# Two Transformer blocks on one core: a second scratch place for the stick-breaking ring, the latent queries' work moved ahead of it, two more modulation tiles in the input projection, and GpSimd's queue no longer emptied in the gather stage

## What is computed

```python
# block 1
proj = rms(x) @ w_in                     # 2208 columns: sb_q, sb_k, sb_v, cq, ckv, k_pe
# stick-breaking attention, 8 heads of 64
z = q k^T / 8;  log_fail = where(s < t, log_sigmoid(-z), 0)
later = cumsum(log_fail, reverse) - log_fail
a = where(s < t, exp(log_sigmoid(z) + later), 0);  sb = a @ v
# latent attention, 8 heads: q = rms(cq) @ w_uq (96 wide), kv = rms(ckv) @ w_ukv
q, k = rms per head; the last 32 of each head turned by rope; softmax over chunks; @ v
x += [rms(sb), rms(mla)] @ w_o
# expert gather: per token 8 heads, top 16 x top 16 of 2 x 128 keys -> 16 experts per head
pre = x . u[idx];  x += sum(softmax(best) * gelu(pre) * v[idx])   # u, v: 16384 x 1024
# block 2
mod = silu(c) @ w_ada + b_ada            # w_ada: 1024 x 6144, one row of six vectors
x += g1 * (mixer(rms(x) * (1 + sc1) + sh1) @ w_out)   # forgetting, mLSTM and block attention
x += g2 * ((silu(gate) * up) @ w_down)
```

## Time and profile before

| | |
|---|---|
| median of 3 runs | 2475.4 us (2469.62 to 2479.81) |
| the profiled execution | 2482.66 us |
| its span, first to last instruction | 2480.7 us |
| mean granted clock of TensorE | 0.905 |
| busy share | PE 84%, DVE 69%, POOL 42%, ACT 25% |
| input projection and what stands before it | 0 to about 136 us |
| up-projection | about 136 to 178 us |
| ring | about 178 to 266 us |
| opening, to the first gather | 266 to 310 us |
| gather stage | 310 to about 1870 us |
| rest of block 2 | to 2480.7 us |

### The profile page before, as it was taken

The page is one execution under the profiler, slowest core; times in us unless marked ns, Lnnn a source line. Parts: engine busy times, 40 slices in busy tenths (PEclk is TensorE's granted clock), DMA queues, the critical chain, the costliest instruction groups (busy, mean ns, idle before and its releaser), DMA issues. The chain is left out here.

```text
span 2480.7 us, 25461 instructions
## 1 busy us (share of the span) xinstructions
PE 2081.8 (84%) x7721; PEld 1317.2 (53%) x7721; DVE 1706.0 (69%) x3528; ACT 610.8 (25%) x1443; POOL 1041.7 (42%) x1086
## 2 busy tenths in 40 slices
PE   7987878987776986877987977777888898999999
PEld 6955555544332343433543433333336874788887
DVE  7747487876877776777666787877856574544464
ACT  3134234432222121122112132222211231210121
POOL 0010066666666666666665666666670000000000
PEclk9985989998887998889999988988998998999999
DMA  7652089999999999999999999999995311333222
GB/s 272 226 196 76 18 307 341 358 366 363 328 330 401 352 371 400 406 387 384 365 403 349 403 397 356 354 362 357 370 376 182 113 44 43 93 101 94 75 86 101
DMA packets 260632, 676.43 MB, mean 273 GB/s; under 512 B 19501, under 2 KB 107938, under 8 KB 260514
## 3 DMA queue, kind: packets, MB, share of 16 engines
q0 software_dynamic: 147456, 536.94, 57.3%
q1 hardware_dynamic: 113058, 138.07, 16.6%
HBM read 672.81 MB, written 2.10 MB: 272 GB/s over the span
## 5 line engine op out<-in xcount | busy, mean ns | idle before, releaser
L2570 PE MATMUL bank<-arena 128*128 128x512 f32 x1568 | 831.9, 666 | 176.1 <-issue 73.2
L2791 DVE SCALAR_TENSOR_TENSOR arena<-arena,h_ps 128x1024 f32<-128x1024 f32 x512 | 612.5, 1217 | 168.0 <-DMA arena<-in_peer_u,arena 116.0
L2524 POOL DMA_INDIRECT arena<-in_peer_v,arena x512 | 512.5, 1001 | 336.1 <-issue 137.8
L2524 POOL DMA_INDIRECT arena<-in_peer_u,arena x512 | 510.1, 996 | 233.5 <-issue 144.3
L2570 PEld LDWEIGHTS bank<-arena 128*128 128x128 f32 x1568 | 311.2, 212 | 539.9 <-issue 428.6
L2805 DVE SCALAR_TENSOR_TENSOR x<-arena,x 128x1024 f32<-128x1024 f32 x120 | 154.4, 1287 | 42.4 <-DMA arena<-in_peer_v,arena 23.6
L2651 ACT ACTIVATE arena<-ident,arena 128x128 f32<-128x128 f32 x392 | 138.5, 393 | 88.9 <-issue 27.7
L142 DVE CAST parts<-arena 128x2048 fp32r<-128x2048 f32 (+5 forms) x61 | 67.6, 1107 | 93.7 <-DMA arena<-in_w_gate_up 75.2
L144 DVE TENSOR_TENSOR parts<-arena,parts 128x2048 fp32r<-128x2048 f32 (+5 forms) x61 | 125.4, 2056 | 4.5
L1605 PE MATMUL bank<-hT,arena 128*128 128x256 f32 (+1 forms) x576 | 122.0, 368 | 3.6 <-DMA arena<-in_peer_w_q 2.2
L1605 PEld LDWEIGHTS bank<-hT,arena 128*128 128x128 f32 x576 | 104.5, 201 | 30.1 <-issue 16.2
(11 more groups left out here) (476 smaller groups left out, 3268.5 us busy)
## 6 DMA issues: line engine op xcount, KB each, us to landing
arena<-in_w_ada SPq DMA_DIRECT2D x12, 2048.0 KB, 12.1
arena<-in_w_in SPq DMA_DIRECT2D x15, 1536.0 KB, 6.8
arena<-in_w_gate_up SPq DMA_DIRECT2D x44, 512.0 KB, 5.0
arena<-in_peer_w_q SPq DMA_DIRECT2D x16, 1024.0 KB, 7.8
arena<-in_w_down SPq DMA_DIRECT2D x22, 512.0 KB, 3.5
arena<-in_peer_u,arena POOLq DMA_INDIRECT x512
arena<-in_peer_v,arena POOLq DMA_INDIRECT x512
arena<-in_w_in SPq DMA_DIRECT2D x7, 1024.0 KB
```

The costliest lines, as they stand in the source:

```text
L2524: nc.gpsimd.indirect_dma_start(out=row, out_offset=None, in_=a[table][0], in_offset=bass.IndirectOffsetOnAxis(ap=expert[:, s % TB, j:j + 1 ...
L2570: ins = nc.tensor.matmul(psum[half][:, :], diag[:, m % R, :], row[:, half * 512:(half + 1) * 512], start=(s % PH == 0 and j == 0), stop=(s ...
L2791: nc.vector.scalar_tensor_tensor(out=u_ring[:, n % R, :], in0=u_ring[:, n % R, :], scalar=1.0, in1=h_ps[:, :], op0=ALU.mult, op1=ALU.mult, ...
```

## The change

1. `ADA_EARLY` goes from 8 to 10: the projection's tiles 3, 4 and 5 carry two `w_ada` tiles each; two are left for the up-projection. There SP issues them ahead of the expert keys, and neither waits for a used place.
2. The queries' work on DVE (`sum_q`, rope, `scale_q` of both groups) moves from the ring's slots to the end of `up_dve`; their root (`root_heads(act, 0)`) moves into `up_act`, behind its 13th sum.
3. The ring's scratch grows from 1024 to 1280 columns; `work0` has two places by turns, so `log_one_plus` waits for the `before_exp` of the unit before the last (group A; `att_b` keeps one).
4. For stick-breaking units of `att_a`, PE issues the scores ahead of the values and the turn in its slot; ACT takes both copies out of PSUM from DVE, and its order in a slot is now log, store, exponents, copy.
5. In the gather stage DVE clears `gate_of[0].bias`, POOL waits for that and does the `iota` alone; the `drain` is gone.

```diff
-        ADA_EARLY = 8
+        ADA_EARLY = 10
-        ADA_AT = {1: (0, 1), 2: (2, 3), 3: (4,), 4: (5,), 5: (6, 7)}
+        ADA_AT = {1: (0, 1), 2: (2, 3), 3: (4, 5), 4: (6, 7), 5: (8, 9)}
@@ up_sync
-            sync.dma_start(key_rows, ...).then_inc(keys_loaded, 16)
             for t in range(ADA_EARLY, ADA_TILES):
                 load_ada(sync, t)
+            sync.dma_start(key_rows, ...).then_inc(keys_loaded, 16)
@@ up_dve
                 ada_weigh(dve, t)
+            sum_q(dve)
+            for g in range(2):
+                turn_q_places(dve, g)
+                add_q_places(dve, g)
+            for g in range(2):
+                scale_q(dve, g)
@@ up_act
+                    if m == 3 * TB:
+                        root_heads(act, 0)
@@ att_places
-            p.work0, p.work1, p.probs, p.probsT = (scratch[:, i * p.n_max:(i + 1) * p.n_max] for i in range(4))
+            p.work1, p.probs, p.probsT, *p.work0 = (scratch[:, at:at + p.n_max] for at in range(0, scratch.shape[-1], p.n_max))
@@ log_one_plus (before_exp takes work0[u % len(p.work0)] likewise)
-            after(act, ready_for_exp, u)
+            after(act, ready_for_exp, u - len(p.work0) + 1)
@@ att_a
-                           psum[0:2], ..., view(DIAG, 1024), False)
+                           psum[0:2], ..., view(DIAG, 1280), False)
@@ att_a_pe
+                scores = due(att_a, slot, 0)
+                scores_first = scores is not None and not unit_of(att_a, scores)[0]
+                if scores_first:
+                    score(att_a, pe, scores)
                 if (u := due(att_a, slot, 6)) is not None:
                     sum_values(att_a, pe, u)
                 if (u := due(att_a, slot, 4)) is not None:
                     turn_probs(att_a, pe, u)
-                if (u := due(att_a, slot, 0)) is not None:
-                    score(att_a, pe, u)
+                if scores is not None and not scores_first:
+                    score(att_a, pe, scores)
@@ att_a_act
+                if (u := due(att_a, slot, 1)) is not None:
+                    log_one_plus(att_a, act, u)
+                if (u := due(att_a, slot, 7)) is not None and not unit_of(att_a, u)[0]:
+                    store_out(att_a, act, nc.scalar.copy, u)
                 if (u := due(att_a, slot, 3)) is not None:
                     exponents(att_a, act, u)
-                if (u := due(att_a, slot, 1)) is not None:
-                    log_one_plus(att_a, act, u)
+                if (u := due(att_a, slot, 5)) is not None and not unit_of(att_a, u)[0]:
+                    copy_probs(att_a, act, nc.scalar.copy, u)
-                if slot in (3, 7):
-                    root_heads(act, slot // 4)
+                if slot == 7:
+                    root_heads(act, 1)
@@ att_a_dve: both copies for latent units alone; sum_q, turn_q_places, add_q_places, scale_q gone
@@ block2_dve, slot I0 + 6 (step 18); the later waits on gates_zeroed count one more
+                dve.wait_ge(q_copied, 2 * PH + 2)
                 dve.wait_ge(sc_summed, 2 * PH + 2)
+                nc.vector.memset(gate_of[0].bias, 0.0).then_inc(gates_zeroed, 1)
                 nc.vector.memset(w_g_a, 0.0).then_inc(gates_zeroed, 1)
@@ gpsimd, step 21
-                            pool.wait_ge(q_copied, 2 * PH + 2)
-                            pool.wait_ge(sc_summed, 2 * PH + 2)
-                            nc.gpsimd.memset(gate_of[0].bias, 0.0)
-                            pool.drain()
+                            pool.wait_ge(gates_zeroed, 1)
                             nc.gpsimd.iota(gate_of[0].bias[0:SM_H, :], ...).then_inc(places_ready, 1)
```

More of the change, by code:

```diff
@@ L1021, in up_sync @@
         def up_sync(sync):
-            sync.dma_start(key_rows, a["peer_sub_keys"][0].rearrange("c h n d -> n (c h) d")).then_inc(keys_loaded, 16)
             for t in range(ADA_EARLY, ADA_TILES):
                 load_ada(sync, t)
+            sync.dma_start(key_rows, a["peer_sub_keys"][0].rearrange("c h n d -> n (c h) d")).then_inc(keys_loaded, 16)
         def up_dve(dve):
@@ L1274, in log_one_plus @@
                 return
-            s, o = p.s_ps[u % len(p.s_ps)][:, 0:n], p.work0[:, 0:n]
+            s, o = p.s_ps[u % len(p.s_ps)][:, 0:n], p.work0[u % len(p.work0)][:, 0:n]
             act.wait_ge(scored, u + 1)
-            after(act, ready_for_exp, u)
+            after(act, ready_for_exp, u - len(p.work0) + 1)
             nc.scalar.activation(o, s, ACT.Abs)
@@ L1292, in before_exp @@
             dve.wait_ge(logged, u // UNITS * (UNITS // 2) + u % UNITS + 1)
-            nc.vector.scalar_tensor_tensor(out=p.work0[:, 0:n], in0=s, scalar=0.0, in1=p.work0[:, 0:n], op0=ALU.max,
-                                           op1=ALU.add)
+            work0 = p.work0[u % len(p.work0)][:, 0:n]
+            nc.vector.scalar_tensor_tensor(out=work0, in0=s, scalar=0.0, in1=work0, op0=ALU.max, op1=ALU.add)
             dve.drain()
             after(dve, probs_ready, u)
-            nc.vector.tensor_tensor_scan(p.work1[:, 0:n][:, ::-1], ones[:, 0:n], p.work0[:, 0:n][:, ::-1], 0.0,
+            nc.vector.tensor_tensor_scan(p.work1[:, 0:n][:, ::-1], ones[:, 0:n], work0[:, ::-1], 0.0,
                                          ALU.mult, ALU.add)
@@ L1356, in program @@
                            [a_pads[:, 512 + i * GT:512 + (i + 1) * GT] for i in range(2)], [view(W_Q + 512 + i * GT, GT) for i in range(2)],
-                           psum[0:2], psum[2], psum[3][:, 0:HD], psum[4], psum[5], view(DIAG, 1024), False)
+                           psum[0:2], psum[2], psum[3][:, 0:HD], psum[4], psum[5], view(DIAG, 1280), False)
+        assert DIAG + 1280 <= SC
         att_b = att_places(1, 4, (0, 1, 2, 3, 4, 5, 6, 7),
@@ L1396, in att_a_dve @@
             for slot in A_SLOTS:
-                if (u := due(att_a, slot, 7)) is not None:
+                if (u := due(att_a, slot, 7)) is not None and unit_of(att_a, u)[0]:
                     store_out(att_a, dve, nc.vector.tensor_copy, u)
-                if (u := due(att_a, slot, 5)) is not None:
+                if (u := due(att_a, slot, 5)) is not None and unit_of(att_a, u)[0]:
                     copy_probs(att_a, dve, nc.vector.tensor_copy, u)
@@ L1402, in att_a_dve @@
                     before_exp(att_a, dve, u)
-                if slot == 0:
-                    sum_q(dve)
                 if slot == 5:
@@ L1407, in att_a_dve @@
                 for g, at in ((0, 2), (1, 18)):
[L1408 to L1413, removed]
                     if slot == at + 7:
@@ L1737, in place_w_g @@
             act.wait_ge(w_2_loaded[0], w_2_count(t))
-            act.wait_ge(gates_zeroed, 1)
+            act.wait_ge(gates_zeroed, 2)
             for at, to, w in ((0, NG + MF, ML_H), (ML_H, MF, ML_H)) if t == 0 else ((0, 0, FOX_H),):
@@ L2218, in block2_act @@
                 else:
-                    act.wait_ge(gates_zeroed, 2)
+                    act.wait_ge(gates_zeroed, 3)
                     conv_load(act, 0, t - 8, psum[t - 3])
@@ L2670, in in_background @@
                         for s, c0 in enumerate((0, SB_W)):
-                            nc.scalar.activation(att_b.work0[:, 0:512], rows[:, tb, c0:c0 + 512], ACT.Square,
+                            nc.scalar.activation(att_b.work0[0][:, 0:512], rows[:, tb, c0:c0 + 512], ACT.Square,
                                                  accum_out=stat[:, s, tb:tb + 1]).then_inc(b_squared, 1)
```

## The result

The kernel before took 2474.3 us (median of 4 runs), the changed kernel 2448.0 us (4 runs, 2444.9 to 2451.6): a ratio of 0.9895, 95% interval 0.9876 to 0.9913, or -26 us. Forecast were 2452.4 us and faster by more than 0.5%. The profiled execution took 2447.7 us for a span of 2445.9 us, 34.8 us less than the span before; that is more than the medians differ by, since the profile of before was 8 us above this median.

A forecast was written before the change was run, and what follows sets the result against it. PE paces the projection, a chain through ACT and DVE the ring, and nearly always busy DMA engines the gathers. The terms, -7.15 - 9.6 - 6.2 = -23.0 us, take the median from 2475.4 to 2452.4 us, range 2443 to 2462.

The forecast's parts named there:

- Input projection: Projection up to the seam: PE sets the pace, DVE's added weighings stay hidden, seam +1.7 us, at 138.1 us.
- Rival (d): Input projection becomes bound by its transfers, so the kernel gets slower: 2484 us at 14 us per tile; chance 0.04.
- Term 1: Up-projection: first ring scores at 173.05 instead of 180.20 us, DVE's queries' work ending last; -7.15 us, seam's 1.7 included.
- Term 2: Ring: pairs of 5.5 us at an unchanged half clock, queries' work gone from the ring; -9.6 us.
- rival (a): Ring: PE's clock returns to 2.4 GHz, pairs take 4.7 us, total 2448 us; chance 0.22.
- Rival (b): Ring: ACT becomes the bound, pair stays near 5.86 us, ring gives only 3.7 us, total 2458.3 us; chance 0.13.
- Term 3: Gather stage: without the emptying of POOL's queue, the hole in DMA time goes; -6.2 us.
- Rival (c): Gather stage: the hole is no loss, gathers behind it are limited elsewhere, gain 0, total 2458.6 us; chance 0.08.
- The sum: Whole kernel: -7.15 - 9.6 - 6.2 = -23.0 us, median 2452.4 us; chance 0.45.

The follow-up runs named there:

- faster group: First and third sets of four runs each, on chips 0 and 5; the kernel before took 2383.1 and 2381.9 us there.
- slower group: Second set of four runs, on chip 12, plus the first pair of profiles; the kernel before took 2475.3 us in that set.
- third set: Four runs on chip 5, timed beside the kernel before at 2381.9 us; the unaltered changed kernel had ratio 0.9915 there.
- first set: Four runs on chip 0, timed beside the kernel before at 2383.1 us; the unaltered changed kernel had ratio 0.9904 there.

## Why the prediction was right, step by step

**Input projection: right, slightly under.** Nothing waits for tiles 4 and 5: the split of tile 4 ended near 95.6 us (predicted 94.4), and TensorE was ready for the tile at 96.25 us, not at the predicted 95.4, so it had 0.6 us to spare. The seam came at +2.4 us where +1.7 were reckoned. The two turns more take 0.85 us each, as reckoned; the rest of the delay is there from the first 20 us on, before any of the added tiles, and the seams of the ten traces with ten tiles spread from 138.4 to 139.5 us by themselves. Rival (d) is out: no transfer is late there, and the median of `w_ada` fell from the 12.1 us of the earlier trace rows:

```profile
arena<-in_w_ada SPq DMA_DIRECT2D x12, 2048.0 KB, 10.0
```

**Term 1, mis-sized: -4.25 us instead of -7.15 us.** The mechanism was right: the first scores of the earlier trace rows came 4.25 us earlier, and VectorE's queries' work ends last. Its two sizes were off. First, the work begins with the squares at 159.07 + 2.77 = 161.84 us, 2.0 later than the predicted 159.8. Of these, 0.7 are the seam's and 1.3 the first twelve sums behind it, 6.84 us instead of the 5.55 of the earlier trace rows. Windows of TensorE behind the seam, first of before and then of the changed kernel, show why:

```profile
136.40:142.00 5.60, 5.60 (x13) 3.29 (x14) 0.00 (x0) 1.73 (x3) 0.90 (x1) 0.74 0.70 186
```

```profile
138.80:144.40 5.60, 5.59 (x9) 3.17 (x10) 0.00 (x0) 1.73 (x2) 0.92 (x1) 0.51 0.80 267
```

The clock was granted at 0.51 in place of 0.74 in the first 5.6 us, behind the same 2.93 us of idle time. This repeats: over the same 5.6 us the four traces with eight tiles in the projection (seam 136.4 to 137.6 us) have 0.70 to 0.74, the ten with ten tiles (seam 138.4 to 139.5 us) 0.50 to 0.60. The prediction priced the sums behind the seam as if the clock there stayed. Second, the work took 13.6 us (161.87 to 175.47) and not 12.7: two rope groups 6.2 instead of 5.8, scalings 3.7 instead of 3.4, and the sum with its small row and handover 3.7 instead of 3.5. The run with this work in the ring starts its scores at 173.02 us: TensorE's own limit there, predicted at 170.6. So the step that the prediction named as the later one really is.

**Term 2, mis-sized: -12.0 us instead of -9.6 us, and partly for another reason.** The whole ring gained 12.0, 11.1 and 12.0 us in the three traces. The prediction had pairs of 5.5 us at a clock that stays at 0.50, which gives 5.5 us over five pairs, and 4.1 us at the opening; measured were 6.6 and 5.35 us. Its price of a pair at half clock was too low: that takes 5.74 us, a gain of only 0.1 us on 5.86 (from the scores' start to the logarithm's it is 1.33 and 0.91 us, where 1.24 and 0.82 were reckoned with the handovers). But the clock didn't stay: it was granted at 0.69, 0.64 and 0.69 over the ring, a pair at 1.00 took 4.72 us, pairs at 0.83 to 0.87 took 4.7 to 5.1 us, and the mean pair between 194.70 and 221.05 us is 5.27 us. That is rival (a) in part: its price of 4.7 us a pair was right, but for a share of the pairs only. The Trainium skill ("TensorE: Matmul & The Clock Gate", Part 1) has the throttled state as the default that activity releases. The traces agree that the ring leaves it at times and falls back, at 0.50 in the earlier trace rows and 0.69 now. Opening the ring goes with a higher clock in every trace: from the first scores to the last exponents the six closed rings have 0.50 to 0.57, the eight opened ones 0.64 to 0.74. Why isn't shown: TensorE was busy for 31.7 of 45 us now and for 32.1 of 45 in the ring put back, at 0.58.

Where the gain comes from was tested. The closed ring takes 57.1 us with the queries' work in it and 51.9 without, so taking that out gives 5.1 us. Opening the chain then gives the other 6.5 us (51.94 less the mean of 45.4), at the higher clock; what it gives at half clock all through wasn't measured, and the 0.1 us of such a pair suggests that it is less. The prediction had it the other way about: 7.8 us from the work (5 x 0.74 + 4.1) and 1.8 from the chain (0.36 us on each of five pairs). Its sum came nearer than its parts.

**Rival (b), ScalarE as the bound of the whole ring, is out.** It is busy for 31.95 of 45 us, up from 16.7 of 38 in the earlier trace rows, and without the copies the ring was no longer and hardly shorter (44.3 us). In the pair at full clock, though, it is busy for 3.97 of 4.72 us, more than any other engine, so rival (a) fully come true would have had rival (b) close behind.

**Term 3, right: -5.5 us measured in the faster group, -6.2 predicted.** Rival (c), the hole is no loss, is out. In the slower group the term isn't measured as well: the removal alone gave -7 us (-3 to -12).

**The sum.** -4.25 - 12.0 puts the first gather at 293.8 us; it is at 294.55. Term 1 gave 2.9 us too little and term 2 gave 2.4 us too much; that the two misses cancel is luck, and the time can't tell it. With the drain that makes -15.5 - 5.5 = -21 us against -23.0 forecast. Measured were -26 us, -24 and -17 us in the three pairs of medians, mean -22.5 us. The -34.8 us between the two profiles consist otherwise: first gather -15.5, gathers -28.8 (1556.0 to 1527.2 us), and the part behind the last gather +9.5 (614.7 to 624.2 us). That last part took 614 to 627 us in the twelve other traces, 616 and 627 in the kernel before and the changed one of the third set, but 614 to 618 in eight others that hold most of the change. The granted clock accounts for most of it: one and the same stretch of 524 matmuls in block 2 took 90.8 us at 0.92 in the first trace of before and 96.2 at 0.86 in that of the changed kernel, 89.0 at 0.94 and 100.3 at 0.82 in the third set, and 89.5 at 0.94 in the changed kernel's trace of the first set. Why the clock was lower in two of the changed kernel's three traces isn't shown. How much of the 28.8 us is the drain's stays open, since only one trace of the slower group has a drain; the five without it took 1527 to 1535 us.

## What to carry to other kernels

A chain that is closed at two places (here a buffer, and the order in a queue) gave nothing until both were opened; undo them one by one before you say which of them paid. Work moved ahead of a stage is worth what it saves in the stage less what it delays its start by: here 4.5 us less 3.1; without the two early tiles the ring started 16 us late. An emptied queue costs the part of its hole that the queued work can't bridge, so look at the transfers' share around it, not at the length of the wait.

## What the runs showed of the hardware that was not expected

The kernel before took 2475 and 2382 us in different sets of runs; most of it lies in the gathers (for the changed kernel 1527 against 1445 us for the same 1024), while the first gather came at the same time within 1 us.

The emptying of GpSimd's queue with gathers queued ahead of it took 19.1 us in the first trace and 18.3 and 16.2 us in the two later ones with it; no emptying ahead of the first gather took more than 2.7 us. In these three traces it ended 2.3, 2.3 and 1.9 us after the last queued transfer had landed, and the next transfer began 2.5 us later still, so no DMA engine moved anything for 4.4 to 4.8 us.

And the same 2.93 us of idle time at the seam was followed by a granted clock of 0.70 to 0.74 in all four traces with the earlier seam and of 0.50 to 0.60 in all ten with the later one.
